# A two-block transformer kernel: a new order of ScalarE's and VectorE's work around the couples of query and key tiles, and one gate tile one step sooner

## What is computed

```python
n = rmsnorm(h, g_mix[l])
aq, ak, av, iq, ik, iw, bq, bk, bv, mq = split_cols_2(n @ w_in[l], IN_SPLITS)
y_a = dsa_attention(aq, ak, av, iq, ik, iw)     # an index score picks 64 keys for each query
y_b = dilated_attention(bq, bk, bv)             # 24 query heads, 24 key heads, three dilations
y_m = memory_attention(mq, rmsnorm(mem, g_mem[l]), w_mem_kv[l])
gates = sigmoid(n @ w_gate[l] + b_gate[l])      # 24 tiles of 128 columns
merged = gates[0] * (y_a @ w_branch[0]) + gates[1] * (y_b @ w_branch[1]) + gates[2] * (y_m @ w_branch[2])

def rope(x):                                    # for queries and keys
    x1, x2 = xf[..., :half], xf[..., half:]
    return concatenate([x1 * cos - x2 * sin, x2 * cos + x1 * sin])
```

## Time and profile before

| | |
|---|---|
| times of the kernel before | median 1037.66 us of 3 (1037.39 to 1039.12) |
| the profiled execution | 1038.44 us, span 1036.6 us |
| PE busy | 1005.3 us, 97% of the span |
| DVE busy | 503.1 us, 49% |
| ACT busy | 353.8 us, 34% |
| PE in the chain that ended last | 86% |
| the couples and what is between them, 497.20 to 573.70 us | PE busy 69.83 of 76.50 us |

### The profile page before, as it was taken

The page is one execution under the profiler, slowest core; times in us unless marked ns, Lnnn a source line. Parts: engine busy times, 40 slices in busy tenths (PEclk is TensorE's granted clock), DMA queues, the critical chain, the costliest instruction groups (busy, mean ns, idle before and its releaser), DMA issues.

```text
span 1036.6 us, 15200 instructions
## 1 busy us (share of the span) xinstructions
PE 1005.3 (97%) x5628; PEld 714.1 (69%) x5628; DVE 503.1 (49%) x1376; ACT 353.8 (34%) x861; POOL 86.1 (8%) x140
## 2 busy tenths in 40 slices
PE   6999999999999999999988999999999999999996
PEld 2468554547887778988988877799998844444442
DVE  5559836456357658656874534853522410000004
ACT  5124134334053246355455123843121411111113
POOL 0060000032100005200000000000000020000000
PEclk9999999999999999999999999999999999999999
DMA  9972125752243331453433342037656799999996
GB/s 366 421 297 83 41 81 211 292 228 82 82 161 124 122 122 63 183 186 125 159 128 136 144 162 96 29 137 327 268 204 282 282 383 421 421 420 420 421 420 251
DMA packets 33941, 227.56 MB, mean 220 GB/s; under 512 B 4577, under 2 KB 4849, under 8 KB 8112
## 3 DMA queue, kind: packets, MB, share of 16 engines
q1 hardware_dynamic: 30784, 214.97, 52.7%
q10 hardware_dynamic: 1920, 9.80, 2.5%
q0 software_dynamic: 1168, 1.85, 0.5%
HBM read 222.15 MB, written 8.41 MB: 222 GB/s over the span
## 4 chain that ended last, share of the span: by engine, by line
PE 86%; DVE 8%; ACT 3%; issue 1%; DMA 1%; DVEq 0%; SPq 0%; ACTq 0%
PE lin L1344 11%; PE sc L671 10%; PE lin L654 8%; PE sc L777 6%; PE aux L1344 5%; PE aux L1231 4%; PE lin L671 4%; PE sc L877 4%; PE lin L841 3%; PE sc L1309 3%; PE sc L654 3%; PE aux L654 3%; PE aux L907 3%; PE sc L1056 2%; PE lin L893 2%; DVE UN L2218 2%
## 5 line engine op out<-in xcount | busy, mean ns | idle before, releaser
L654 PE MATMUL lin<-H,ring 128*128 128x256 f32 (+1 forms) x560 | 126.1, 386 | 0.7 <-ACT PR L1809 0.7
L654 PEld LDWEIGHTS lin<-H,ring 128*128 128x128 f32 x560 | 105.9, 190 | 19.1 <-issue 4.2
L777 PE MATMUL sc<-H,ring 128*128 128x512 f32 (+1 forms) x192 | 67.3, 496 | 0.0
L1557 ACT ACTIVATE SP<-lin 128x512 f32<-128x512 f32 (+2 forms) x88 | 42.1, 486 | 71.9 <-PE lin L893 71.9
L2218 DVE SCALAR_TENSOR_TENSOR UN<-UN,cols 128x512 f32<-128x512 f32 (+1 forms) x120 | 66.7, 626 | 0.0
L2130 DVE CUSTOM_DVE_ANT_0 SP<-sc,CW,SK 128x512 f32<-128x512 f32 (+1 forms) x48 | 31.7, 661 | 53.6 <-PE sc L877 53.6
L1568 ACT ACTIVATE SP<-SP,ST 128x513 f32<-128x513 f32 (+4 forms) x88 | 53.9, 612 | 6.7 <-DVE ST L2133 6.4
L777 PEld LDWEIGHTS sc<-H,ring 128*128 128x128 f32 x192 | 34.8, 189 | 30.3 <-issue 25.6
L2728 DVE TENSOR_TENSOR PR<-lin,PR 128x512 f32<-128x512 f32 x8 | 5.5, 692 | 94.6 <-PE lin L1344 94.6
L877 PE MATMUL sc<-PR 64*128 64x256 f32 (+3 forms) x240 | 42.2, 434 | 2.9 <-DVE ST L2130 2.1
L1231 PE MATMUL aux<-Y,ring 128*128 128x256 f32 x192 | 41.8, 379 | 0.0
(11 more groups left out here) (491 smaller groups left out, 1870.6 us busy)
## 6 DMA issues: line engine op xcount, KB each, us to landing
ring<-w_stream SPq DMA_DIRECT2D x119, 1024.0 KB, 6.6
SP<-w_stream SPq DMA_DIRECT2D x14, 1024.0 KB, 20.7
UN<-w_stream SPq DMA_DIRECT2D x10, 1024.0 KB, 19.6
PR<-w_stream SPq DMA_DIRECT2D x8, 1024.0 KB, 17.8
CW<-w_stream SPq DMA_DIRECT2D x8, 1024.0 KB, 16.5
X<-w_stream SPq DMA_DIRECT2D x8, 1024.0 KB, 17.1
Y<-w_stream SPq DMA_DIRECT2D x8, 1024.0 KB, 18.6
PR<-ada_in SPq DMA_DIRECT2D x5, 1024.0 KB, 26.5
```

The lines of the kernel that those rows point to most:

```text
L654: m = mm(dst, w[:, k, :], rhs(k), start=n == 0, stop=n == KT - 1)
L777: m = mm(bank[:, 0:ns * SEQ], filling["w"][:, k, :], H[:, 0:ns, k, :], start=k == 0, stop=k == KT - 1)
L1557: fn(PT[:, g % TURNED, a:b], take()[:, 0:b - a], ACT.Copy).then_inc(lin_taken, 1)
```

## The change

Four things are done. (1) In a couple that begins at `t`, ScalarE turns the two plain tiles before it (`t`-2, `t`-1) no longer behind their copies but inside the couple: one behind the reads of P1, the other behind the reads of P3. VectorE rotates them there too, and the two weight mixes of the next couple stand in other places of its order. (2) Of the four turns of the couple's own tiles, two stay behind its last read and two go behind the copy of the plain tile that follows. (3) Four of the eight rounds and the mask move from the steps 13 to 17 to the steps 32 to 35, and the first values' mix from step 36 to step 32. (4) The second gate tile moves from step 4 to step 3 of the attention.

```diff
-GATE_STEPS = (1, 4, 7, 10, 13, 16, 40, 42)
+GATE_STEPS = (1, 3, 7, 10, 13, 16, 40, 42)
...
                         fn(b_tiles(c, x)[0][0], b_banks(c, x)[0], ACT.Copy).then_inc(quarter_read, 1)
+                    act.wait_ge(lin_taken, turn["in2", t - 1] + 1)
+                    half_turned(PR[:, AT[t - 2], :]).then_inc(half_in, 1)
                     for x in range(2):
                         act.wait_ge(quarter_made, b_at(c, x, 6))
                         fn(b_tiles(c, x)[1][0], b_banks(c, x)[0], ACT.Copy).then_inc(quarter_read, 1)
+                    half_turned(PR[:, AT[t - 1], :]).then_inc(half_in, 1)
...
-                    for x in range(2):
-                        act.wait_ge(quarter_read, b_read(c, x, 4))
-                        half_turned(PR[:, AT[t + 2 * x], :]).then_inc(half_in, 1)
...
-                    if t in ROPED2:
+                    if t in ROPED2 and t + 1 not in COUPLES and t + 2 not in COUPLES:
                         ins = half_turned(bank)
                     ins.then_inc(lin_taken, 1)
+                    if t - 4 in COUPLES:
+                        c = COUPLES.index(t - 4)
+                        for x in range(2):
+                            act.wait_ge(quarter_read, b_read(c, x, 4))
+                            half_turned(PR[:, AT[t - 4 + 2 * x], :]).then_inc(half_in, 1)
...
+                    turned = len(ROPED1) + 6 * c
+                    rope(None, PR[:, AT[t - 2], :], t2("cos"), t2("sin"), True, turned=turned + 1)
                     if c + 1 < len(COUPLES):
                         mixed_queries(c + 1, 0)
+                    rope(None, PR[:, AT[t - 1], :], t2("cos"), t2("sin"), True, turned=turned + 2)
...
-                if t == BV:
+                if t == MQ[0]:
                     mixed_values(0)
...
-                if BQ + 1 <= t < BQ + 1 + TOPK // 8:
+                if BQ + 1 <= t < BQ + 5 or MQ[0] <= t < MQ[0] + 4:
```

More of the change, by code:

```diff
@@ L2387, in _ @@
                         v.tensor_tensor(to, to, B_Z[:, x, :], ALU.add).then_inc(quarter_added, 1)
+                    if c + 1 < len(COUPLES):
+                        mixed_queries(c + 1, 1)
                     for x in range(2):
@@ L2393, in _ @@
                     for n, tile in enumerate((t + 1, t + 3, t, t + 2)):
[L2394 to L2397, removed]
+                        rope(None, PR[:, AT[tile], :], t2("cos"), t2("sin"), True, turned=turned + n + 3)
+                elif any(a - 3 < t < a + 4 for a in COUPLES):
                     pass
@@ L2481, in _ @@
                         after(step(v.match_replace(x, M8[:, tt, :], x, GONE)))
-                if t == BQ + 1 + TOPK // 8:
+                if t == MQ[0] + 3:
                     for tt in range(TT):
```

## The result

| | before | after |
|---|---|---|
| median | 1037.54 us of 4 (1037.39 to 1039.12) | 1027.53 us of 4 (1027.24 to 1028.39) |
| ratio | | 0.9901, interval 0.9884 to 0.9919 |
| the profiled execution | 1038.44 us, span 1036.6 | 1028.39 us, span 1026.6 |

In a later series of runs the same two kernels had medians of 1038.46 and 1027.36 us, ratio 0.9894 (0.9878 to 0.9911). So the change wins 10.0 to 11.1 us. Why that number itself wavers is a part of what follows.

The account below looks back on a forecast made before the run. TensorE, busy 97% of the span, was taken as the bound. Couples' 10.60 us (7.30 waiting, 3.30 slow clock) plus the gate tile's 0.50 made 11.1, so the median 1037.66 becomes 1026.6 us; range 1024.9 to 1030.6.

Parts of the forecast that it names:

- the list: ScalarE's placed reads, turns and copies in a couple starting at T; no TensorE wait for L1782 left.
- P6's margin: In a couple, ScalarE's reads over at T+8.0, TensorE starts P6 at T+9.05: smallest margin, 1.05 us.
- The undisturbed couple: Length of a couple without waits, taken from the first couple: 13.60 us less 0.93 lost, 12.67 us.
- the order closes a circle: Rival, couples: a turn waits for a rotation behind a VectorE mix, stalling TensorE; margin 3.9 us, 1040 us; slower, chance 0.03.
- The 0.93 us: First couple: P3's wait for VectorE's mix goes, as a key-search round of 1.69 us ahead of it goes.
- The lateness among the values: Values: VectorE's first addition comes 4.4 us late, with 3.3 us to spare before the second group's mix.
- Cost nothing: Values: four rounds and the mask moved there, 8.0 us of VectorE work, cost no time.
- The 3.30 us: Second and third couple: slow matmuls behind the gaps, 1.65 us each, counted as won within the 10.60.
- the clock's part is not there: Rival: timed runs mostly lack slow stretches, only 7.3 + 0.5 us won, 1029.9 us; chance 0.11.
- The gate tile: Attention start: fills the 1.05 us wait before pair 2's scores; 0.5 us won, ends 0 and 1.05.
- What follows moves forward as a whole.: Behind the stretch to the last stage: later loads follow TensorE's semaphores and TensorE waits for no DMA, so all moves.
- The sum: Whole kernel: 10.60 + 0.50 = 11.1 us won, profiled execution 1027.3, median 1026.6 us; chance 0.76.

Follow-up runs that it names:

- all but the gate tile: Changed kernel with the second gate tile back at step 4 of the attention: 1028.13 us (1027.82 to 1030.0, 5 runs).
- the rounds back: Changed kernel with all eight rounds of the key search and the mask back at steps 9 to 17: 1030.46 us (1029.73 to 1030.67, 4 runs).
- The lighter loads: Last 12 units bring half their weights: 1027.45 us in the changed kernel, 1038.47 in the kernel before.

## Why the prediction was right, and where it was not

**The turns (ScalarE).** Right, in every time of the list. The reads, the turns and the copies stand within 0.2 us of where they were placed, and L1782 and L1787 have no wait of TensorE behind them. P6's margin was put at 1.05 and is 1.1 us: in the second couple the first of P4's two reads ends at 524.84, and P6 begins at 525.92, two quarter products behind P5 at 524.13. The undisturbed couple was put at 12.67 and is 12.59. Undoing the two moves singly gives back 3.90 and 1.00 us, together 4.64. No run undoes VectorE's new order of mixes and rotations by itself, so its own share is not shown.

**The smallest margin.** Here a step was missing. The prediction called P6's the smallest, and placed the last two additions at T+12.4 and ScalarE's turns at T+13.2 without setting the one against the other. In the trace 0.2 us lie between the end of these additions (510.31) and the turns (510.53). It held, so the forecast is not touched, but the rival "the order closes a circle" was underpriced. Its margin of 3.9 us is the rotation's. By way of the additions three rounds on VectorE were enough to lose 1.6 us in the second couple.

**The first couple, the rounds, the values.** The 0.93 us went. Expected was the last mix at 500.9, it came at 501.06. The lateness among the values was put at 4.4, with 3.3 to spare, and the runs with more work on VectorE show 3.5. "Cost nothing" held. But what the moved rounds earn was mis-sized, if one reads the prediction as 0.93 for the first couple: in the new order of the turns they are worth 3.0 us (68.42 against 65.39).

**The slow clock.** The 3.30 us were right for the one execution and only in part for the kernel. Three profiles of the couples of before, from the first couple's start to the values', have 76.35, 74.76 and 74.75 us, with two slow stretches, the second only and the first only. The rows of the experiments give the same account in another way: 65.39 changed, plus 4.64 for the turns, plus 3.03 for the rounds, is 73.06, plus one stretch of 1.65 is 74.71, plus two is 76.36. This takes it that the parts add and leaves nothing for VectorE's new order. The times fit: 35 later executions of the kernel before in three series lie at 1036.8 to 1037.8 us (14 of them) or at 1038.05 to 1039.97 (21), with a granted clock over the whole execution of 0.996 or 0.997 in the lower group and of 0.994 or 0.995 in the upper (0.996 in one). Only a profile shows the stretches themselves, so that the groups are those with one and with two is read from the times and not shown. So the rival "the clock's part is not there" was right in its reason: part of the 3.30 is there in part of the executions. The same gap of 2.0 or 3.2 us is followed by a slow stretch in two of the three profiles and by none in the third. The Trainium skill ("TensorE: Matmul & The Clock Gate", section "The HAM clock gate") has the gate's watch free-running. The three profiles agree with it. What is won is 9.4 us of the couples where before had one stretch and 11.0 where it had two, and the gate tile's 0.7: 10.0 to 11.7 us.

**The gate tile.** Right in kind: the wait ahead of pair 2's scores gone, a new one ahead of pair 3's. It was put at 0.5 us, 0.5 for the new wait, and it measured 0.7 and 0.41. At the scores of pair 3 0.5 us are won, as forecast (613.22 - 562.83 = 50.39 behind the values' start, where before had 624.40 - 573.52 = 50.88). The other 0.2 are at the turned probabilities behind them, which take 0.63 us from start to start (613.87 to 614.50) and took 0.84 before; the prediction had nothing there.

**"What follows moves forward as a whole."** This step failed for the profiled execution. The prediction looked at TensorE's waits in the last stage and found no DMA. VectorE's was not looked at. Before the change it had waited 5.65 us for the rows' read-back and ended its row additions at 1027.05 us. Four additions of TensorE's products come behind them, for the last of which TensorE's product was ready at 1029.34. Done without a pause they take 2.48 us, as in the changed kernel, so the last one could have begun at 1028.9: the row additions had some 0.45 us to spare. In the changed kernel the read-back was issued 11.68 us sooner, 0.33 more than TensorE moved, and landed 1.8 us later after its issue. 1.8 - 0.33 - 0.45 is 1.0, and VectorE's last addition of a product ends 1.04 us later behind TensorE's last matmuls than before (1019.75 - 1015.99 = 3.76, and 2.72). Another 0.26 are lost among VectorE's few operations behind it. So 1.3 us of the gain were gone in that execution. In the one looked at next the 1.04 were not, and 0.2 were.

**The numbers.** The sum was 11.1 us. TensorE's last matmuls moved by 11.35: 10.96 in the couples and 0.68 at the gate tile, less 0.27 by which the first couple began later in this execution (497.44 and 497.17), to within 0.02. The profiled executions moved by 10.05 (1038.44 to 1028.39) and by 11.22 with the second profile of the changed kernel (1027.22). The median was put at 1026.6 and is 1027.53, because, by this account, the median of before, 1037.54, lies in the lower group of its times, that of one slow stretch, and the sum took two from it: 1037.5 - 9.4 - 0.7 = 1027.4.

Left open is why the read-back lands after 8.9 to 11.3 us in one execution and 12.2 to 14.7 in another. Of the ten profiles of kernels with full loads and the new order or most of it, three have VectorE's last addition late because of it, by 1.0, 2.0 and 0.6 us (the changed kernel, all but the gate tile, the rounds back), and seven by less than 0.1. The lighter loads show that it does not set the median, not what disturbs it.

## What to carry to other kernels

A long list of an engine whose results others wait for is best broken where that engine waits anyway: here ScalarE's turns cost nothing between reads for which it has to wait for TensorE, and 3.9 us ahead of them. For each new order write down the margin of every pair "needed by, made at", not only those on the bounding engine, and carry out the subtraction; the smallest one here stood in the list and was not subtracted. A slow stretch behind a gap is a matter of chance for each execution, so take its price from several profiles before it enters a sum.

## What the runs showed of the hardware

- The slow clock behind a gap of TensorE, among the couples and the values: in no profile behind gaps of 0.59 to 1.36 us, in two of three behind 2.0 us and in two of three behind 3.2 us, and in the one with 3.59 us. Its cost hardly depends on the gap: 1.65 us behind 2.0 and 3.2 us, 1.76 behind 3.59.
- Four transfers of 512 KB behind a stream that fills the DMA engines (DMA share 0.99 to 1.03 and 407 to 429 GB/s from 1000 to 1005 us) landed 8.9 to 14.7 us after their issue in the same place of kernels that hardly differ, and after 3.5 to 6.8 us with half of each of the last 12 loads taken away.
